# Odd and end stages of a two-layer streaming encoder: x in three loads, y in three parts, U turned from T, causal masks made later in place

## The chip, the cores and the metric

The program runs on one core of one Trainium2 chip. The metric is the device time of one execution in microseconds (us); lower is better. All arrays are float32. TensorE multiplies float32 operands as they are (a product of two float32 tiles is recorded as two matmuls), and operands that were rounded to the `fp32r` form as one.

## The reference

One inference step of a two-layer encoder on 320 tokens: 256 of a prompt and 64 of a sample, in chunks of 64. The width is 1024.

```python
def _swiglu(h, wg, wu, wd):
    return (jax.nn.silu(h @ wg) * (h @ wu)) @ wd        # 1024 -> 2816 -> 1024
# layer 0: x += 0.5 * swiglu(rmsnorm(x)); x += mix_even(rmsnorm(x)); x += 0.5 * swiglu(rmsnorm(x))
# layer 1: x += 0.5 * swiglu(rmsnorm(x)); x += mix_odd(rmsnorm(x));  x += 0.5 * swiglu(rmsnorm(x))
```

`mix_even` is a sparse softmax attention beside a gated linear attention; the change doesn't touch it. `mix_odd` is a gated delta rule with 8 heads of 128. In it, for each chunk of 64 tokens and each head:

```python
decay = jnp.exp(jnp.where(incl, gcum[..., :, None] - gcum[..., None, :], -jnp.inf))
lower = jnp.where(strict, jnp.einsum('bhtd,bhsd->bhts', kb, kc) * decay, 0.0)
sol = lax.linalg.triangular_solve(eye + lower, rhs, left_side=True, lower=True, unit_diagonal=True)
attn = jnp.where(incl, jnp.einsum('bhtd,bhsd->bhts', qc, kc) * decay, 0.0)
```

What follows is a recurrence over the chunks with the state of each head.

## The kernel before

x is held turned, as xT with the 1024 features in 8 tiles of 128 partitions and the 320 tokens along a row. Five engines run their own instruction streams, written out by hand and tied by semaphores: SyncE (SP) issues the loads of weights, ScalarE (ACT) rounds each weight tile to a high part, VectorE (DVE) or GpSimd (POOL) subtracts to get the low part, and TensorE (PE) does each product as three matmuls: high by high, high by low, low by high (L592 to L594 in the four FFNs, L677 to L679 in the odd layer's input projection).

**Start.** `prologue` on SP loads x of the prompt in one DMA (L521) and of the sample in another (L522), both counted by one semaphore, then gate and up weights of tile 0; the second pair waits until eleven small parameter rows have landed. PE waits for the whole of x, turns it with 24 transposes (L572), then turns the parameter rows (L576 to L578). ACT copies all six banks to xT, then the parameters, then rounds the gate weights, then makes h_hi (L1399). DVE makes h_lo (L1840) and the low weight parts (L1828). The first FFN's row norm needs the sum of squares over the features: ACT squares (L1405) and DVE sums the 8 tiles in one reduction (L1882) behind the low parts of weight tile 1. PE's `norm` (L587) stands between the products of weight tiles 0 and 1 and waits for that sum.

**Odd layer.** PE's loop over 32 weight tiles t is `project_odd(t)` and, behind it, pieces of the delta rule. T is the inverse of (1 + lower) and U is T turned; both are kept. Each of the five chunks starts from a first 2x2 level and is refined five times, which gives 25 steps m (chunk m % 5, level m // 5). A step is: Y = level mask of L times U (`inverse_y`, L1111, in bank 4), ACT copies Y (`y_out`), then T -= Y' T in bank 6 (L1126) and U -= T' Y in bank 7 (L1133), in `inverse_tu`; DVE subtracts both (`update`, L2315 and L2317). In the last level (m of 20 to 24) only U is refined. Steps stand one to a t at t = 14 to 23, two to a t at 24 to 28, and the rest at 29 to 31.

POOL makes for each t the low weight parts (`split_mix`, L2517) and masks (`masked`, L2586): the causal mask of the decays Dm into a tile At of its own at t = 11 to 15, the first level of T at t = 12 to 16 (`lev0`), and the level mask of step m = t - 12, which goes over Dm, so it waits for the causal mask. DVE's `lower` (L2285) reads Dm, `first_t` (L2291) waits for the first level, and `queries` (L2303) multiplies At at t = 19 to 23. PE's `key_products` (L1073, L1074) waits for `lower` of the chunk before, and `first_inverse` (L1097) turns T for the first U.

**End.** The last FFN's down product runs over 8 output tiles; DVE adds each to xT (L1868, L1872). Then `epilogue`: PE waits for the last tile and turns all of xT (24 transposes, L1253), ACT copies six banks to ytok (L1279), and POOL stores y of the prompt and of the sample in two DMAs (L2457) and waits for them.

## Time and profile before

| what | value |
|---|---|
| median of 3 timed runs | 1511.71 us (1511.51 to 1513.51) |
| profiled execution, device time | 1505.85 us |
| its span, first to last instruction | 1504.1 us |
| mean granted TensorE clock | 0.98 of full |
| PE busy | 1436.9 us (96% of the span) |
| DVE, ACT, POOL busy | 879.3, 603.3, 355.9 us |

Busy time is the time in which an engine has an instruction under way; a matmul's record begins before the one ahead ends, so the distance from start to start is what one costs in a row of them. Idle time in brackets stands before the instruction and names what ended it. The granted clock is 1.00 at 2.4 GHz and 0.50 at 1.2 GHz. The profiled execution is 5.86 us below the median of the timed runs.

### The profile page before, as it was taken

The numbers are of one execution on the slowest core, as the hardware profiler recorded it, in microseconds if no ns is written. First come the engines' busy times: TensorE is split into PE (matmuls) and PEld (weight loads), VectorE is DVE, ScalarE is ACT, GpSimd is POOL, SyncE is SP. The second block draws the span as 40 slices with busy tenths as digits, with TensorE's granted clock in tenths as the row PEclk, the third lists the DMA queues.
The fourth block names the chain that finished last, engine by engine and source line by source line (L and its number), as shares of the span: only waits on it lengthen the run. The fifth ranks groups of instructions, "written<-read, shape, count | busy, mean of one in ns | idle before, by whom it ended". The sixth has DMA issues, their size and how long they took to land.

```text
span 1504.1 us, 25482 instructions
## 1 busy us (share of the span) xinstructions
PE 1436.9 (96%) x9830; PEld 1400.1 (93%) x9830; DVE 879.3 (58%) x1388; ACT 603.3 (40%) x990; POOL 355.9 (24%) x341
## 2 busy tenths in 40 slices
PE   6999998999879999999999999999999889999997
PEld 5999998899868999999999999988999779999997
DVE  4666653477755666655666655667564456666641
ACT  5333323546533533332533332557432544333321
POOL 3000023656205200003100002549465242000000
PEclk8999999999979999999999999989999999999999
DMA  7655951344402455774455674212221222555751
GB/s 182 167 140 149 279 145 31 112 121 126 134 1 76 126 160 142 201 186 106 114 162 143 172 215 115 81 59 85 79 63 57 87 85 82 160 150 140 182 154 35
DMA packets 323307, 188.21 MB, mean 125 GB/s; under 512 B 10874, under 2 KB 320632, under 8 KB 323244
## 3 DMA queue, kind: packets, MB, share of 16 engines
q1 hardware_dynamic: 321088, 181.95, 43.9%
q0 software_dynamic: 1568, 5.29, 1.2%
q8 instruction: 42, 0.69, 0.2%
q10 hardware_dynamic: 588, 0.12, 0.0%
q14 instruction: 21, 0.17, 0.0%
HBM read 183.22 MB, written 4.11 MB: 125 GB/s over the span
## 4 chain that ended last, share of the span: by engine, by line
PE 87%; DVE 6%; ACT 4%; issue 2%; POOL 1%; DMA 0%; ACTq 0%; SPq 0%
PE PS L592 21%; PE PS L593 20%; PE PS L594 20%; PE PS L677 2%; PE PS L679 2%; PE PS L678 2%; PE PS L1133 1%; PE PS L1111 1%; PE PS L696 1%; PE PS L650 1%; PE PS L697 1%; PE PS L698 1%; PE PS L651 1%; PE PS L652 1%; PE PS L1126 1%
## 5 line engine op out<-in xcount | busy, mean ns | idle before, releaser
L592 PE MATMUL PS<-h_hi,w_parts 128*128 128x320 f32 x1408 | 438.8, 312 | 7.8 <-DVE h_lo L1840 7.8
L594 PE MATMUL PS<-h_hi,w_parts 128*128 128x320 f32 x1408 | 436.5, 310 | 0.0
L593 PE MATMUL PS<-h_lo,w_parts 128*128 128x320 f32 x1408 | 436.5, 310 | 0.0
L592 PEld LDWEIGHTS PS<-h_hi,w_parts 128*128 128x128 f32 x1408 | 265.9, 189 | 9.6 <-issue 7.9
L593 PEld LDWEIGHTS PS<-h_lo,w_parts 128*128 128x128 f32 x1408 | 265.9, 189 | 0.4 <-issue 0.2
L594 PEld LDWEIGHTS PS<-h_hi,w_parts 128*128 128x128 f32 x1408 | 265.6, 189 | 0.0
L1279 ACT ACTIVATE w_parts<-gu 128x1024 fp32r<-128x1024 f32 x176 | 176.7, 1051 | 160.2 <-PE PS L594 159.0
L1828 DVE TENSOR_TENSOR w_parts<-gu,w_parts 128x1024 fp32r<-128x1024 f32 x176 | 209.0, 1228 | 16.4 <-ACT w_parts L1279 16.2
L592 PE MATMUL PS<-act_hi,w_parts 128*128 128x320 f32 x704 | 217.5, 309 | 0.0
L593 PE MATMUL PS<-act_lo,w_parts 128*128 128x320 f32 x704 | 217.5, 309 | 0.0
L594 PE MATMUL PS<-act_hi,w_parts 128*128 128x320 f32 x704 | 217.5, 309 | 0.0
L2517 POOL TENSOR_TENSOR w_mix<-gu,w_mix 128x512 fp32r<-128x512 f32 x116 | 154.5, 1343 | 124.0 <-ACT w_mix L1279 123.8
L1279 ACT ACTIVATE w_parts<-dn 128x1408 fp32r<-128x1408 f32 x64 | 84.8, 1373 | 183.6 <-PE PS L594 183.6
L592 PEld LDWEIGHTS PS<-act_hi,w_parts 128*128 128x128 f32 x704 | 132.2, 188 | 0.0
L593 PEld LDWEIGHTS PS<-act_lo,w_parts 128*128 128x128 f32 x704 | 132.2, 188 | 0.0
L594 PEld LDWEIGHTS PS<-act_hi,w_parts 128*128 128x128 f32 x704 | 132.2, 188 | 0.0
L1392 ACT ACTIVATE rs<-rs 128x320 f32<-128x320 f32 x88 | 41.5, 472 | 203.0 <-DVE rs L1853 203.0
L1828 DVE TENSOR_TENSOR w_parts<-dn,w_parts 128x1408 fp32r<-128x1408 f32 x64 | 118.3, 1888 | 7.3 <-ACT w_parts L1279 7.1
L2505 POOL TENSOR_TENSOR RB<-xT 128x320 f32<-128x320 f32 x5 | 3.6, 721 | 495.2 <-DVE xT L1872 482.2
L1279 ACT ACTIVATE w_mix<-gu 128x512 fp32r<-128x512 f32 x116 | 72.0, 630 | 121.1 <-PE PS L679 68.2
L1859 DVE TENSOR_TENSOR rs<-rs,PS 128x320 f32<-128x320 f32 x88 | 42.9, 487 | 130.5 <-PE PS L594 130.1
L1868 DVE TENSOR_TENSOR rs<-PS,RB 128x320 f32<-128x320 f32 x32 | 15.7, 491 | 144.5 <-PE PS L594 144.5
(378 smaller groups left out, 2383.7 us busy)
## 6 DMA issues: line engine op xcount, KB each, us to landing
gu<-in_ffn_w_gate SPq DMA_DIRECT2D x88, 512.0 KB, 4.0
gu<-in_ffn_w_up SPq DMA_DIRECT2D x88, 512.0 KB, 5.2
dn<-in_ffn_w_down SPq DMA_DIRECT2D x32, 1408.0 KB, 7.1
gu<-in_od_w_in SPq DMA_DIRECT2D x32, 512.0 KB, 5.1
gu<-in_ev_w_in SPq DMA_DIRECT2D x26, 512.0 KB, 4.8
dn<-in_ev_w_out SPq DMA_DIRECT2D x4, 1024.0 KB, 5.3
dn<-in_od_w_out SPq DMA_DIRECT2D x4, 1024.0 KB, 5.0
RB<-bias_rows POOLq DMA_DIRECT2D x2, 576.0 KB, 7.7
```

What stands on the lines that cost most here:

```text
L592: mm(out, w_hi, hi, start=first, stop=False)
L593: mm(out, w_hi, lo, start=False, stop=False)
L594: return mm(out, w_lo, hi, start=False, stop=last)
L677: mm(out, w_hi, h_hi[:, k, :], start=(k == 0), stop=False)
L678: mm(out, w_hi, h_lo[:, k, :], start=False, stop=False)
L679: ins = mm(out, w_lo, h_hi[:, k, :], start=False, stop=(k == KT - 1))
L1279: return act_(out, in_, ACT.Copy, scale=scale)
L1392: act_(tanh_g[:, slot, :], gated[:, slot, :], ACT.Tanh, scale=0.5).then_inc(tanh_done, 1)
L1828: tt(w_parts[:, slot, 1, w], raw[:, slot, w], w_parts[:, slot, 0, w].bitcast(F32), ALU.subtract)\
L1859: tt(gated[:, slot, :], gated[:, slot, :], bank(2 * slot + 1, T), ALU.mult).then_inc(act_done, 1)
L1868: tt(tanh_g[:, slot, :], bank(4 + slot, T), rstd, ALU.mult).then_inc(act_mid, 1)
L2517: po.tensor_tensor(mix_parts(n, t)[:, 1, w].rearrange("p (k c) -> p k c", k=4), raw[:, 4 * half:4 * half + 4, :], mix_parts(n, t)[:, 0, w] ...
```

## The change

x comes in three loads with a semaphore each, and PE turns each part as it lands. The six banks are copied by ACT (lower halves) and DVE (upper halves). The 32 FFN gains get a semaphore, a transpose and a bank of their own, and the other parameters are copied later. ACT rounds the first gate weights behind two tiles of h_hi; DVE sums the squares with three adds, ahead of weight tile 1, and `norm` adds the last two tiles on PE. In the odd layer `inverse_tu` becomes `inverse_t`, which keeps one product a step, and `inverse_turn`, two steps later, which turns T into U for m below 20; DVE copies U from bank 7. The level masks get a tile of their own (where Dm was), Dm moves to where At was, and the causal mask is made in place at t = 17 to 21. At the end xT is turned in three parts: tiles 0 to 3 ahead of the last down product, 4 to 6 in its middle, 7 behind it; SP stores the three parts of the prompt and two of the sample, and ACT the last of the sample.

```diff
-            sp.dma_start(xnat[:, 0:2, :], I["x_prompt"][0].rearrange("(i p) d -> p i d", p=P)).then_inc(x_in, 16)
-            sp.dma_start(xnat[0:TS, 2, :], I["x_sample"][0]).then_inc(x_in, 16)
+            for i in range(2):
+                sp.dma_start(xnat[:, i, :], I["x_prompt"][0, i * P:(i + 1) * P, :]).then_inc(x_in[i], 16)
+            sp.dma_start(xnat[0:TS, 2, :], I["x_sample"][0]).then_inc(x_in[2], 16)
             load_gu(0)
-            sp.wait_ge(params_in, 16 * 11)
+            sp.wait_ge(params_in, 16 * 10)
...
+            for evacs, c0, c1 in ((11, 0, 512), (14, 512, 896)):
+                sp.wait_ge(pro_evac, evacs)
+                store(y_rows[:, :, c0:c1], ytok[:, :, c0:c1])
+                store(O["y_sample"][0][:, c0:c1], ysample[0:TS, c0:c1])
+            sp.wait_ge(pro_evac, 16)
+            store(y_rows[:, :, 896:D], ytok[:, :, 896:D])
...
             def prologue():
                 pe.wait_ge(consts, 1)
-                pe.wait_ge(x_in, 32)
                 for i in range(3):
+                    pe.wait_ge(x_in[i], 16)
...
-                pe.wait_ge(params_in, 16 * 11)
+                pe.wait_ge(gains_in, 16)
+                tr(bank(7)[:, 0:32], rs[0:32, 0:P], ident[0:32, 0:32]).then_inc(pro_pe, 1)
+                pe.wait_ge(params_in, 16 * 10)
...
                     pe.wait_ge(first_total, 1)
-                else:
-                    pe.wait_ge(total_ready, r)
+                    mm(bank(6, T), ones[:, :], squares[:, 0, :], start=True, stop=False)
+                    mm(bank(6, T), ones[:, :], squares[:, 1, :], start=False, stop=True).then_inc(norm_sum, 1)
+                    return
...
+                        if m == KT - 1 and k == FT // 2:
+                            turn_out(1)
...
+                if f == 3:
+                    down(0, KT - 2, 0)
+                    turn_out(0)
+                    down(1, KT - 1, 0)
+                    turn_out(2)
...
+            def turn_out(part):
+                tiles = (range(0, 4), range(4, 7), range(7, 8))[part]
+                pe.wait_ge(x_upd, X_FFN[3] + 3 + tiles[-1])
+                if part == 2:
+                    pe.wait_ge(pro_evac, 11)
+                for i in range(3):
+                    rows = P if i < 2 else TS
+                    for k in tiles:
+                        ins = tr(bank(y_bank(part, i))[0:rows, (k - tiles[0]) * P:(k - tiles[0] + 1) * P],
+                                 xT[:, k, i * P:i * P + rows], ident[:, :])
+                    ins.then_inc(pro_pe, 1)
...
-                        inverse_tu(t - 14)
+                        inverse_t(t - 14)
+                    if 16 <= t < N_CONV:
+                        inverse_turn(t - 16)
...
                             if m < 25:
-                                inverse_tu(m)
+                                inverse_t(m)
+                            if m - 2 < 4 * NCH:
+                                inverse_turn(m - 2)
...
+            def inverse_t(m):
                 c = m % NCH
                 pe.wait_ge(o["y_evac"], m + 1)
                 if m >= NCH:
                     pe.wait_ge(o["t_upd"], m - NCH + 1)
+                if m:
+                    pe.wait_ge(o["t_upd"], m)
+                else:
+                    pe.wait_ge(o["kt_evac"], NCH)
+                for p in range(C_PAIRS):
+                    left, right = yT[:, m % 2, p, :], tT[:, c, p, :]
+                    if m >= 4 * NCH:
+                        left, right = right, left
+                    ins = mm(bank(6)[:, p * P:(p + 1) * P], left, right, start=True, stop=True)
+                ins.then_inc(o["t_pe"], 1)
+            def inverse_turn(m):
+                pe.wait_ge(o["t_upd"], m + 1)
                 if m:
                     pe.wait_ge(o["u_upd"], m)
                 else:
                     pe.wait_ge(o["u1_evac"], 2)
                 for p in range(C_PAIRS):
-                    ins = mm(bank(7)[:, p * P:(p + 1) * P], tT[:, c, p, :], yT[:, m % 2, p, :], start=True, stop=True)
+                    ins = tr(bank(7)[:, p * P:(p + 1) * P], tT[:, m % NCH, p, :], ident[:, :])
                 ins.then_inc(o["u_pe"], 1)
...
# ACT
+                    sc.wait_ge(pro_pe, 2 * i + 1)
+                    copy(xT[:, 0:4, i * P:i * P + n_], bank(2 * i).rearrange("p (k c) -> p k c", k=4)[:, :, 0:n_])\
+                        .then_inc(pro_evac, 1)
...
+                        if f == 0 and k == 1:
+                            split_gate_up(0, 0, 0, 0, (0,))
...
                 if f == 0:
                     split_gate_up(0, 0, 0, 0, (1,))
+                    other_params()
...
                 def y_out(m):
                     sc.wait_ge(o["y_pe"], m + 1)
                     if m >= 2:
-                        sc.wait_ge(o["u_pe"], m - 1)
+                        sc.wait_ge(o["t_pe"], m - 1)
...
# DVE
+                if f == 0:
+                    low_parts(0, gain, range(2))
+                    split_half(0, gu, 0, 0, 0, 0)
+                    low_parts(0, gain, range(2, KT))
+                    split_half(0, gu, 0, 0, 0, 1)
+                    for j in range(1, 4):
+                        ve.wait_ge(sq_done, j + 1)
+                        ins = tt(squares[:, 0:2, :], squares[:, 0:2, :], squares[:, 2 * j:2 * j + 2, :], ALU.add)
+                        if j < 3:
+                            link(ins)
+                    ins.then_inc(first_total, 1)
...
+                def inverse_update(m):
                     c = m % NCH
+                    matrix = (tT if m < 4 * NCH else uT)[:, c, :, :]
+                    ve.wait_ge(o["t_pe"], m + 1)
+                    tt(matrix, matrix, bank(6).rearrange("p (a c) -> p a c", a=4), ALU.subtract).then_inc(o["t_upd"], 1)
+                def u_turned(m):
                     ve.wait_ge(o["u_pe"], m + 1)
+                    cp(uT[:, m % NCH, :, :], bank(7).rearrange("p (a c) -> p a c", a=4)).then_inc(o["u_upd"], 1)
...
# POOL
-                masked(Dm[:, c, :, :], Lm[:, c, :, :], lev[:, m // NCH + 1:m // NCH + 2, :], o["bm"])
+                masked(level[:, c, :, :], Lm[:, c, :, :], lev[:, m // NCH + 1:m // NCH + 2, :], o["bm"])
...
-                if 11 <= t < 16:
-                    c = t - 11
-                    po.wait_ge(o["dexp"], c + 2)
-                    masked(At[:, c, :, :], Dm[:, c, :, :], maskI.unsqueeze(1), o["am"])
...
                 if 12 <= t < N_CONV:
-                    if t < 17:
-                        po.wait_ge(o["am"], t - 11)
                     level_mask(t - 12)
+                if 17 <= t < 22:
+                    masked(At[:, t - 17, :, :], Dm[:, t - 17, :, :], maskI.unsqueeze(1), o["am"])
...
```

## Rows read from the trace of the kernel before

**Rows 1.** The page: share of the chain that ended last, by engine.

```profile
PE 87%; DVE 6%; ACT 4%; issue 2%; POOL 1%; DMA 0%; ACTq 0%; SPq 0%
```

**Rows 2.** Timeline of the start: start us, length us, engine, line, idle before.

```profile
7.75 4.31 PE L572 MATMUL PS<-ident,RA 128*128 128x128 f32 x24 [7.75 <-DMA RA<-in_x_sample]
13.91 1.25 DVE L1828 TENSOR_TENSOR w_parts<-gu,w_parts 128x1024 fp32r<-128x1024 f32 x1 [13.91 <-ACT w_parts L1279]
15.77 0.61 PE L592 MATMUL PS<-h_hi,w_parts 128*128 128x320 f32 x1 [3.37 <-DVE h_lo L1840]
21.24 0.47 PE L594 MATMUL PS<-h_hi,w_parts 128*128 128x320 f32 x1
21.51 0.38 PE L592 MATMUL PS<-h_hi,w_parts 128*128 128x320 f32 x1
...
24.18 4.53 DVE L1882 TENSOR_REDUCE RB<-RA 128x320 f32<-128x2560 f32 x1
25.24 0.31 PE L593 MATMUL PS<-h_lo,w_parts 128*128 128x320 f32 x1
25.39 0.31 PE L594 MATMUL PS<-h_hi,w_parts 128*128 128x320 f32 x1
28.85 1.41 PE L587 MATMUL PS<-RB,ones 128*128 128x320 f32 x2 [3.15 <-DVE RB L1882]
29.59 0.94 PE L592 MATMUL PS<-h_hi,w_parts 128*128 128x320 f32 x1
```

**Rows 3.** DMA issues: operation, engine, count, size, us from issue to landing.

```profile
gu<-in_ffn_w_up SPq DMA_DIRECT2D x1, 512.0 KB, 8.7
out_p_gla<-RB POOLq DMA_DIRECT2D x1, 128.0 KB, 2.2
out_y_sample<-RA POOLq DMA_DIRECT2D x1, 256.0 KB, 4.9
```

**Rows 4.** Odd layer, chain of waits in order of time: start, length, engine, line.

```profile
1122.33 0.89 PE PS L1111 x8
1123.27 1.13 PE PS L1126 x8
...
1165.67 0.87 PE PS L1145 x8
```

**Rows 5.** Stretches: length, busy us of PE, PEld, DVE, ACT, POOL, granted clock, DMA, GB/s.

```profile
29.00:34.00 5.00, 5.00 (x24) 4.61 (x25) 0.82 (x2) 3.11 (x5) 0.00 (x0) 0.71 1.06 235
1050.00:1080.00 30.00, 30.00 (x241) 29.99 (x240) 18.56 (x38) 13.00 (x31) 17.53 (x14) 1.00 0.24 71
1079.00:1084.00 5.00, 5.00 (x25) 5.00 (x25) 0.17 (x1) 0.96 (x2) 1.28 (x1) 0.66 0.00 0
```

**Rows 6.** DVE groups of 1008 to 1187 us: busy, mean ns, idle before.

```profile
L2315 DVE TENSOR_TENSOR RA<-RA,PS 128x512 f32<-128x512 f32 x20 | 13.7, 683 | 12.4 <-PE PS L1133 12.3
```

**Rows 7.** Timeline of POOL, DVE and PE in the odd layer.

```profile
1022.55 1.32 POOL L2586 TENSOR_TENSOR RB<-RB 128x512 f32<-128x512 f32 x1
...
1030.97 0.49 PE L1073 MATMUL PS<-RB 128*128 128x128 f32 x2 [0.77 <-DVE RB L2285]
1038.11 0.49 PE L1073 MATMUL PS<-RB 128*128 128x128 f32 x2 [1.59 <-DVE RB L2285]
1038.58 1.75 DVE L2291 TENSOR_TENSOR RA<-ident,RA 128x512 f32<-128x512 f32 x1 [0.52 <-POOL RA L2586]
1045.73 0.63 PE L1097 MATMUL PS<-ident,RA 128*128 128x128 f32 x4 [1.17 <-DVE RB L2285]
...
1169.41 1.13 PE L1111 MATMUL PS<-RB 128*128 128x128 f32 x8 [1.08 <-issue]
```

**Rows 8.** Timeline of the end.

```profile
1491.60 0.49 DVE L1868 TENSOR_TENSOR rs<-PS,RB 128x320 f32<-128x320 f32 x1 [8.66 <-PE PS L594]
1496.66 0.74 POOL L2457 DMA_DIRECT2D out_y_prompt<-RA  x1 [238.33 <-ACT RA L1279]
1497.40 0.55 POOL L2457 DMA_DIRECT2D out_y_sample<-RA  x1
```

More of the change, by code:

```diff
@@ L324, in mix_parts, with y_bank @@
             return w_mix[:, t % 2, :, :]
+        def y_bank(part, i):
+            return ((0, 1, 2), (3, 6, 7), (0, 1, 2))[part][i]
         def odd_bank(t):
@@ L1245, in recurrence @@
                 turn(NCH - 1, 1)
-            def epilogue():
-                pe.wait_ge(x_upd, X_FFN[3] + 2 + KT)
-                for i in range(3):
-                    rows = P if i < 2 else TS
-                    for half in range(2):
-                        for k in range(4):
-                            ins = tr(bank(2 * i + half)[0:rows, k * P:(k + 1) * P],
-                                     xT[:, 4 * half + k, i * P:i * P + rows], ident[:, :])
-                        ins.then_inc(pro_pe, 1)
             prologue()
@@ L1263, in _ @@
             ffn(3)
-            epilogue()
         @block.scalar
@@ L1299, in prologue, with other_params @@
                     n_ = P if i < 2 else TS
-                    for half in range(2):
-                        sc.wait_ge(pro_pe, 2 * i + half + 1)
-                        copy(xT[:, 4 * half:4 * half + 4, i * P:i * P + n_],
-                             bank(2 * i + half).rearrange("p (k c) -> p k c", k=4)[:, :, 0:n_]).then_inc(pro_evac, 1)
+                    sc.wait_ge(pro_pe, 2 * i + 1)
+                    copy(xT[:, 0:4, i * P:i * P + n_], bank(2 * i).rearrange("p (k c) -> p k c", k=4)[:, :, 0:n_])\
+                        .then_inc(pro_evac, 1)
                 sc.wait_ge(pro_pe, 7)
-                copy(cols[:, 0:C_QN], bank(6, 222)[:, 0:C_QN])
+                copy(cols[:, 0:32], bank(7, 32)).then_inc(pro_evac, 1)
+            def other_params():
+                sc.wait_ge(pro_pe, 8)
+                copy(cols[:, 32:C_QN], bank(6, 222)[:, 32:C_QN])
                 copy(cols[:, C_QN:C_QN + 1], bank(6, 222)[:, C_QN:C_QN + 1], A_D ** -0.5)
@@ L1770, in epilogue @@
             def epilogue():
-                for i in range(3):
-                    n_ = P if i < 2 else TS
-                    for half in range(2):
-                        sc.wait_ge(pro_pe, 7 + 2 * i + half + 1)
-                        copy(ytok[0:n_, i, half * 512:(half + 1) * 512], bank(2 * i + half)[0:n_, :])\
+                for part, c0, c1 in ((0, 0, 512), (1, 512, 896)):
+                    for i in range(3):
+                        sc.wait_ge(pro_pe, 8 + 3 * part + i + 1)
+                        n_ = P if i < 2 else TS
+                        copy((ytok[:, i, c0:c1] if i < 2 else ysample[0:TS, c0:c1]), bank(y_bank(part, i))[0:n_, 0:c1 - c0])\
                             .then_inc(pro_evac, 1)
+                sc.wait_ge(pro_pe, 16)
+                copy(ytok[:, :, 896:D], banks(0, 2, P)).then_inc(pro_evac, 1)
+                sc.wait_ge(pro_evac, 16)
+                sc.dma_start(O["y_sample"][0][:, 896:D], ysample[0:TS, 896:D]).then_inc(y_out, 16)
             prologue()
-            split_gate_up(0, 0, 0, 0, (0,))
             ffn(0, C_FFN, 0)
@@ L2345, in odd @@
                     if 14 <= t < N_CONV:
-                        update(t - 14)
+                        inverse_update(t - 14)
+                    if 16 <= t < N_CONV:
+                        u_turned(t - 16)
                     if t in (17, 18):
@@ L2355, in odd @@
                             if m < 25:
-                                update(m)
+                                inverse_update(m)
+                            if m - 2 < 4 * NCH:
+                                u_turned(m - 2)
                 gate_silu(31)
@@ L2436, in _ @@
             ve.sem_inc(act_split, 2)
-            split_half(0, gu, 0, 0, 0, 0)
+            for i in range(3):
+                n_ = P if i < 2 else TS
+                ve.wait_ge(pro_pe, 2 * i + 2)
+                cp(xT[:, 4:8, i * P:i * P + n_], bank(2 * i + 1).rearrange("p (k c) -> p k c", k=4)[:, :, 0:n_])\
+                    .then_inc(pro_evac, 1)
             ffn(0, C_FFN)
```

62 lines of the change are left out of this document (24 added, 38 removed).

## The prediction

> **What bounds the kernel now.** The chain of waits gives PE 87% of the span and every other engine together 11% [rows 1], so time is to be had in two ways: work taken off PE where it runs without a gap, and gaps of PE closed. I read the timeline of the first 40 us and of the last 15, then busy time by stretches of the odd layer, then the timeline of each engine where PE has gaps there. The reader is to see three places.
>
> At the start PE waits until 7.75 for the whole of x, again 3.37 us until 15.77, and 3.15 us at 28.85 for the sum of squares [rows 2]. From 15.77 matmuls stand 0.27 apart (21.24 to 21.51) and later 0.15 (25.24 to 25.39) [rows 2]; the first is the clock at 1.2 GHz. After the wait at 28.85 it is low again: the mean grant of 29 to 34 is 0.71, which is 2.9 of 5 us at half [rows 5].
>
> In the odd layer PE is busy all of 1050 to 1080 us, DVE 18.56 of 30 and POOL 17.53 [rows 5]: what leaves PE there leaves the span. Only before 1046 has it gaps, 0.77, 1.59 and 1.17 us, each behind DVE's `lower` [rows 7]; DVE in turn sits in `first_t` until POOL's mask (1038.58, idle 0.52 [rows 7]), and POOL has three masks of about 1.3 us and two weight parts for each t.
>
> At the end nothing overlaps: the last product ends at 1491.55, DVE starts at 1491.60, POOL issues y at 1496.66 and 1497.40 [rows 8], the last lands 4.9 later [rows 3], at 1502.3, and the span closes 1.8 after that.
>
> **The change, part by part.** Minus is faster.
>
> *x in three loads, copies on two engines.* What ended the second wait was not x but the order on ACT: six copies, parameters, gate rounding, then h_hi. With x0 landing first (1 MB lands 5.5 after issue, so half of it near 5) PE turns it before x1 is there, at the same 4.31 us for 24 [rows 2] spread over the landings, ends near 9.2, and ACT, with three copies instead of six, has two tiles of h_hi by about 10.7. Next it wants the weights, and waits for both halves of them: up was issued at 2.56 and lands 8.7 later, 11.3 [rows 3]. SP now has one more x DMA of about 0.5 us ahead, but the DMA engines are full until 10.6, so I put landing at 11.4 (bounds 11.3 and 11.8). Then rounding 1.1, DVE's low part 1.25 [rows 2] and two semaphore steps: PE starts at 13.95 instead of 15.77, **−1.8** (bounds −1.4 and −2.1). The low tiles 2 to 7 of h come 0.45 apart where PE takes 0.8 a tile, so they are not late. SP's second weight pair waits for ten parameter rows and not eleven, the last of them the same one as before: nothing.
>
> *Sum of squares.* The reduction of 4.53 stood behind two low parts of 1.2 [rows 2]. Now three adds of 640 elements, about 0.9 each by the 128x320 operations of 0.49 [rows 8], follow the squares as they come and end near 20.6. PE ends weight tile 0 at 13.95 + 9.8 = 23.7, so the wait is gone: 25.54 to 28.85, **−3.3**. `norm` is two float32 products instead of one: the one cost 28.85 to 29.59, 0.74 at the low clock [rows 2], so two at the high clock cost 0.74: nothing. Without the gap the clock should not fall; PE was slow for 2.1 us of the products behind 29.59, **−1.0** (bounds 0 and −1.4). What is late next: rstd, at 24.4 + 2.3 = 26.8, the activation of tile 0 by 29.5 and the low half of tile 2 by 31.1, against PE's need of it at 31.5. That is 0.4 to spare; if it is missed, some tenths. Start in all: **−6.1** (−3.5 to −7).
>
> *U turned from T.* A product of a step is 0.89 [rows 4]; four transposes are half of the eight in 0.87, 0.44 [rows 4]. Products go from 45 (20 of T, 25 of U) to 25, transposes of T come in for 20 of the steps: 20 x 0.89 = 17.8 off, 20 x 0.44 = 8.7 on, of which one 0.44 falls in the gap of 1.08 at t = 29 [rows 7]. **−9.5**. At 24 to 28, where two steps share a t, the second T product came 0.05 late and took 1.13 for 0.89 [rows 4], since DVE's update of T waited for U's product as well. Now DVE starts a semaphore (0.2 to 0.3) after T's product, takes 0.68 [rows 6], and PE has a turn and a Y, 1.33, in between: five times 0.27, **−1.3**. DVE trades a subtraction of 0.68 for a copy of about 0.69 of the same shape: nothing. The new wait, `inverse_turn` for T's update, stands two steps behind it; behind it in PE's queue are the next projection and the next Y, and Y wants the U of five steps ago, copied in the t before, 3.5 us of projection earlier. The price of these waits lies between 0 and, if each t lost the 1.33 between DVE and PE, +20; I take 0, since each is released a t earlier.
>
> *Causal masks later.* POOL loses one mask of 1.32 [rows 7] at each of t = 11 to 15, where it was late, and gets it at 17 to 21, where its load by t becomes 4 x 1.28 = 5.1 against PE's 6.65. DVE's `first_t` comes up to 1.4 earlier, but ACT's two table loads at t = 12 and its own order let only 0.46 through to `lower(2)` and 0.93 to `lower(4)`. Of the gaps 0.77 shrinks to 0.31 and 1.17 to 0.70; the 1.59 stays: **−0.9** (bounds 0 and −3.5, all three gaps). Odd layer in all: 9.5 + 1.3 + 0.9 = **−11.7** (−6 to −14).
>
> *y in three parts.* 21 of 24 transposes move ahead of the last product's end: 21 x 0.109 [rows 4] = +2.3, a move only. From that end: DVE 1.1, three transposes 0.5, a copy 0.5, a semaphore, issue at +2.3; the last store is 128 KB, which took 2.2 elsewhere [rows 3], ACT's small one a little more: +4.7, against 10.75 before (1491.55 to 1502.3). 4.7 − 10.75 + 2.3 = **−3.8** (−2.5 with a landing of 3.5; −4.5 at the best). The first two parts are copied and stored under the last product, 9.7 us long.
>
> *A rule against it.* The 0.109 apart of L1145 is the rate of a full clock, and PE came to those transposes from products [rows 4]; the trace has no stretch made mostly of them. The Trainium skill (TensorE: Matmul & The Clock Gate, Part 4: PE-mode transpose) says that a transpose doesn't count as activity of PE for the clock gate. By that rule the added ones invite falls of the clock; by the rows they don't, and the sum stays. I keep the rule's case as a rival.
>
> **The sum.** −6.1 − 11.7 − 3.8 = −21.6 on 1505.85, the profiled execution, which gives 1484.3. The median of the runs lies 5.86 higher; no part of the change should alter what lies between, so I predict 1511.7 − 21.6 = **1490 us**, 1.4% less.
>
> **Rivals.**
> 1. *PE isn't the bound in the odd layer once its load is less.* Then the shorter steps turn into waits for DVE, whose own work by t is about 5.5 us, or for ACT's copies of Y. For: PE did wait for DVE before 1046 [rows 7]. Against: 18.56 of 30 busy [rows 5]. Half of −9.5 lost and −0.9 too: 1490 + 5.7, about 1496.
> 2. *The start gives only its first part.* The clock stays low longer after an earlier, cold start, or rstd is late for tile 2: of −6.1 some −2.5 is left, and y's landing is 1 us longer: about 1494.5.
> 3. *The clock falls oftener.* After the 20 one-column sums before 1079 the mean grant of 1079 to 1084 was 0.66 [rows 5], which costs 5 x 0.34 = 1.7. If the turns bring a fall at each t of 16 to 31, 16 x 1.7 = 27 more: 1490 + 27 = 1517, slower. It decides from 13 falls on. For: the clock did fall in a busy stretch. Against: products stay most of each t. One or two falls more or less, at either sign, are likely: ±3.4.
> 4. *The change doesn't do what it says*, some moved wait ends where the old one did in all three places: no change, 1511.
>
> **How the numbers follow.** Forecast 0.68 (its own range 1486 to 1495), rival 1 0.13, rival 2 0.13, rival 3 0.03, rival 4 0.03. Less than 0.2%, 3 us, can't be told from no change here. Faster 0.94, same 0.03, slower 0.03. The range for 8 in 10 goes from the best bounds with a fall of the clock less, 1484, to rival 1 with a fall more, 1499.
>
> **What would show it.** The first product near 14, `norm` with no wait and the next product near 24.4; L1133 gone, t = 24 to 28 about 8.0 apart instead of 9.2, and 14 to 23 0.45 to 0.9 shorter; PE's three gaps before 1046 down by about 0.9 together; stores issued 2.3 after the last product and a span that ends 6.5 after it instead of 12.6. Waits of PE for DVE or ACT in the odd layer at t of 16 on, or low clock there in new places, would make it wrong.

## The result, and the profile after

The changed kernel takes 1484.24 us (median of 4 runs, 1483.85 to 1486.27) against 1511.76 for the kernel before, a ratio of 0.9829 [0.981, 0.9849]. The profiled execution took 1483.85 us, 22.0 less than the profiled one of before (1505.85): the sum of the prediction was 21.6. The medians differ by 27.5. The 5.5 between the two figures are not shown to be the change's work, and they have experiments of their own below.

The page of the changed kernel, its span, the share of PE, and the chain by engine: PE's share of the chain goes from 87% [rows 1] to 89%, and PE is busy for 96% of the span.

```profile
span 1482.1 us, 25338 instructions
PE 1427.7 (96%) x9753; PEld 1391.3 (94%) x9753; DVE 877.1 (59%) x1394; ACT 602.1 (41%) x989; POOL 356.7 (24%) x339
PE 89%; DVE 5%; ACT 4%; issue 2%; DMA 0%; ACTq 0%
```

**The start** (timeline of the changed kernel: start, length, engine, line, idle before). It answers to [rows 2].

```profile
4.70 4.14 PE L590 MATMUL PS<-ident,RA 128*128 128x128 f32 x24 [4.70 <-DMA RA<-in_x_prompt]
11.50 1.06 ACT L1320 ACTIVATE w_parts<-gu 128x1024 fp32r<-128x1024 f32 x1 [1.15 <-DMA gu<-in_ffn_w_up]
12.59 1.23 DVE L1878 TENSOR_TENSOR w_parts<-gu,w_parts 128x1024 fp32r<-128x1024 f32 x1 [1.64 <-ACT w_parts L1320]
13.91 0.60 PE L614 MATMUL PS<-h_hi,w_parts 128*128 128x320 f32 x1 [2.84 <-issue]
17.82 2.54 DVE L1932 TENSOR_TENSOR RA<-RA 128x640 f32<-128x640 f32 x3
22.94 0.70 PE L605 MATMUL PS<-RA,ones 128*128 128x320 f32 x2
23.78 0.55 PE L614 MATMUL PS<-h_hi,w_parts 128*128 128x320 f32 x1
```

PE turns the first part of x at 4.70 where it stood until 7.75; the first product is at 13.91 for 15.77. The three adds end at 20.4, before PE asks at 22.94, so `norm` waits for nothing, and the next product stands at 23.78 for 29.59. A mark below is the start of the same group of PE's instructions in two traces. Every later mark up to the odd layer is 6.8 to 6.9 earlier than before (the even layer's first turn 257.4 to 250.6, first odd projection 961.6 to 954.7). Some tenths of that belong to the execution: a second profiled execution of the changed kernel (experiment 8) has its first turn of the even layer at 251.3, one of the kernel before (experiment 1) at 258.1.

**The odd layer** (timeline of PE in the changed kernel at one t of the second half: Y, T, turn, Y, T, turn; then two of DVE's groups of 990 to 1171 us, with busy time, mean ns, idle before). Before, a step had a T and a U product, each of the size of the Y product of 0.89 [rows 4].

```profile
1129.09 1.05 PE L1157 MATMUL PS<-RB 128*128 128x128 f32 x8
1129.98 1.06 PE L1174 MATMUL PS<-RA,dn 128*128 128x128 f32 x8
1130.87 0.60 PE L1185 MATMUL PS<-ident,RA 128*128 128x128 f32 x4
1131.31 1.06 PE L1157 MATMUL PS<-RB 128*128 128x128 f32 x8
1132.42 1.13 PE L1174 MATMUL PS<-RA,dn 128*128 128x128 f32 x8
1133.38 0.60 PE L1185 MATMUL PS<-ident,RA 128*128 128x128 f32 x4
```

```profile
L2373 DVE COPY RB<-PS 128x512 f32<-128x512 f32 x20 | 13.6, 682 | 0.0
L2369 DVE TENSOR_TENSOR RA<-RA,PS 128x512 f32<-128x512 f32 x20 | 13.6, 679 | 4.7 <-PE PS L1174 4.7
```

The turn takes 0.44 (1130.87 to 1131.31), as its price said, and no wait stands ahead of it. DVE's copy of U costs 0.682 where a subtraction of that shape cost 0.683 [rows 6]. But the second T product of this t still starts late: Y ends at 1131.31 + 0.89 = 1132.20, T starts at 1132.42. It waits for DVE's update of T, and that one stood behind DVE's product of the output gate (timeline of DVE at this place):

```profile
1130.37 1.30 DVE L2281 SCALAR_TENSOR_TENSOR RB<-RA,RB 128x320 f32<-128x320 f32 x1 [0.59 <-ACT RA L1706]
1131.60 0.67 DVE L2369 TENSOR_TENSOR RA<-RA,PS 128x512 f32<-128x512 f32 x1
```

The T product ahead had ended at 1130.87. The same holds at two more of the five t; at one where DVE is free in time (update at 1106.60) the second T product starts without a wait. The t of 24 to 28 stand 8.0 to 8.3 apart, for 9.15 before. Before, PE had three gaps ahead of 1046, of 0.77, 1.59 and 1.17 us [rows 7]; now it has one:

```profile
1029.96 0.49 PE L1119 MATMUL PS<-RB 128*128 128x128 f32 x2 [1.37 <-DVE RB L2341]
```

From the first odd projection to the first new values the odd layer takes 212.1 us instead of 224.7, −12.6. The lead of the changed kernel is 6.89 at the first key product (1015.40 to 1008.51), 9.45 at the second Y (1046.19 to 1036.74), ahead of which no product of U stands, and 19.48 at the first new values: 2.6 are the masks' part and 10.0 that of U. Behind it a little is given back. Two stretches of the recurrence in the changed kernel (length, busy us of PE, PEld, DVE, ACT, POOL, granted clock, DMA, GB/s), and the only one of the kernel before, at 1226:

```profile
1168.00:1172.00 4.00, 3.98 (x26) 3.21 (x28) 1.02 (x3) 1.67 (x6) 0.00 (x0) 0.57 0.67 227
1206.00:1214.00 8.00, 6.55 (x28) 6.55 (x29) 1.56 (x4) 0.50 (x2) 0.46 (x1) 0.57 0.46 133
```

```profile
1226.00:1230.00 4.00, 4.00 (x17) 4.00 (x18) 0.00 (x0) 0.00 (x0) 0.00 (x0) 0.57 0.55 160
```

The lead is 19.5 at the first new values (1186.3 to 1166.9), 18.5 at the recurrence's last turn and 17.6 at the last FFN's products (1413.5 to 1395.9): 1.9 lost, across the two stretches at 1.2 GHz.

**The end** (timeline of the changed kernel, then its last DMA issues with size and us to landing). It answers to [rows 8].

```profile
1476.31 0.49 DVE L1918 TENSOR_TENSOR rs<-PS,RB 128x320 f32<-128x320 f32 x1 [10.96 <-PE PS L616]
1477.38 0.55 PE L673 MATMUL PS<-ident,xT 128*128 128x128 f32 x3 [1.11 <-DVE xT L1922]
1477.86 0.38 ACT L1320 ACTIVATE RB<-PS 128x256 f32<-128x256 f32 x1 [5.81 <-PE PS L673]
1478.28 0.38 SPq L568 DMA_DIRECT2D out_y_prompt<-RB  x1
1478.29 0.54 ACTq L1827 DMA_DIRECT2D out_y_sample<-hT  x1
```

```profile
out_y_prompt<-RB SPq DMA_DIRECT2D x1, 128.0 KB, 1.9
out_y_sample<-hT ACTq DMA_DIRECT2D x1, 32.0 KB, 2.1
```

From the last product (1476.27) the stores are issued after 2.0, land after 2.1 more, and the span ends at 5.9, where it was 12.6. Less the 2.3 of turns moved ahead of the product, that is −4.4.

By stages the 22.0 are: start −6.9, odd layer −12.6, given back +1.9, end −4.4.

### The profile page after: what moved, and what is told of

Same layout as the page of the kernel before. It is cut to its first block, busy times and chain, and to the rows that moved or that the text cites. A ratio compares the mean times of both kernels' runs of the same rounds, so it can differ in the third digit from the quotient of the medians.

```text
span 1482.1 us, 25338 instructions
## 1 busy us (share of the span) xinstructions
PE 1427.7 (96%) x9753; PEld 1391.3 (94%) x9753; DVE 877.1 (59%) x1394; ACT 602.1 (41%) x989; POOL 356.7 (24%) x339
## 4 chain that ended last, share of the span: by engine, by line
PE 89%; DVE 5%; ACT 4%; issue 2%; DMA 0%; ACTq 0%
PE PS L614 21%; PE PS L616 21%; PE PS L615 21%; PE PS L719 2%; PE PS L721 2%; PE PS L720 2%; PE PS L1174 2%; PE PS L1157 2%; PE PS L738 1%; PE PS L692 1%; PE PS L739 1%; PE PS L740 1%; PE PS L693 1%; PE PS L694 1%; DVE RA L2061 1%
## 5 line engine op out<-in xcount | busy, mean ns | idle before, releaser
L614 PE MATMUL PS<-h_hi,w_parts 128*128 128x320 f32 x1408 | 437.8, 311 | 7.2 <-DVE h_lo L1890 4.4
```

What stands on the lines that cost most here:

```text
L614: mm(out, w_hi, hi, start=first, stop=False)
```

## The experiments

Times are medians; "low" is the lowest of a kernel's runs. The kernel before ran 65 times over all comparisons: 19 executions took 1505.4 to 1507.5 us and 46 took 1510.5 to 1515, none between. The changed kernel ran 9 times: 1483.8 to 1488.1. The experiments ran on three chips (1 to 4 and 12 on one, 5 to 8 on a second, 9 to 11 on a third); each comparison had the kernel before on its own chip, with executions of both groups every time. Differences below are to the changed kernel's median of 1484.24, so where the two ran on different chips they carry that too. "Loss" is the time that PE had less of full clock: a fall of 3.4 us at 1.2 GHz is a loss of 1.7. The "even tail" of the expectations is the end of the even layer, about 375 to 484 us.

**1. The kernel before, unaltered.**

> The kernel before, unchanged, once more. The timed runs of before lie 5.9 us above its profiled execution (1511.71 against 1505.85), those of the changed kernel only 0.4 (1484.24 against 1483.85), so of the 27.5 us between the medians the two traces explain 22.0. Theory 1: the 5.9 us are inside the span, in executions in which something of the kernel before runs slower (the clock, a stage); then the spans of the timed runs are near 1510 and differ from 1504, and the profile taken here may show where. Theory 2: they lie outside the span (between launch and first instruction); then spans are near 1504 in all runs and only the device time differs, by 5 to 6 us more than the usual 1.7.

Measured 1511.42 (1506.43 to 1514.75, 12 runs), ratio 1.0003 [0.9987, 1.0018]; profiled execution 1511.56, with a span of 1509.8. The time outside the span is 1.7, as in the shorter ones (1505.85 with 1504.1), so the 5.7 lie inside. The marks agree within 0.9 up to the first turned values of the even tail (393.11 and 393.94), and differ by 5.8 from 425 on. Stretch 396 to 408 of the shorter execution, then of this one (granted clock behind POOL's column):

```profile
396.00:408.00 12.00, 11.13 (x94) 10.66 (x95) 11.20 (x28) 6.18 (x15) 2.73 (x4) 1.00 0.23 75
```

```profile
396.00:408.00 12.00, 10.99 (x58) 10.83 (x58) 7.80 (x18) 5.21 (x13) 1.27 (x2) 0.57 0.28 94
```

PE is as busy and does 58 instructions for 94, at 0.57: one fall of the clock more (396 to 406, 5.1 of loss), in the even layer, far from the change; the fall behind it is longer by 1.7. The prediction's 5.86 was a second group of executions, not a fixed part.

**2. U by a product again.** In `inverse_turn`'s place a product, at once and not two steps later, and DVE subtracts as before:

```diff
-                            if m - 2 < 4 * NCH:
-                                inverse_turn(m - 2)
+                            if m < 4 * NCH:
+                                inverse_turn(m)
...
-                pe.wait_ge(o["t_upd"], m + 1)
...
-                    ins = tr(bank(7)[:, p * P:(p + 1) * P], tT[:, m % NCH, p, :], ident[:, :])
+                    ins = mm(bank(7)[:, p * P:(p + 1) * P], tT[:, m % NCH, p, :], yT[:, m % 2, p, :], start=True, stop=True)
```

> The changed kernel with U refined by a product again (20 products of 0.89 in place of 20 turns of 0.44, DVE subtracts and waits for both products). By the sum of the prediction +9.5 and +1.3, so 10.8 slower than the changed kernel, near 1495. By rival 1 (PE is not the bound once its load is less) only about 5 slower, near 1489.

Measured 1496.05 (1495.74 to 1497.76, 6 runs), ratio 0.9907 [0.9888, 0.9926]: +11.8 on the changed kernel; between the profiled executions +12.3, of which the odd layer has +11.4. Of these, 1.5 came ahead of the first step, with a fall at 996 us that the changed kernel has not; 9.9 are left for U. PE of this kernel, at the same place as the T and turn above:

```profile
1131.79 1.06 PE L1173 MATMUL PS<-RA,dn 128*128 128x128 f32 x8
1132.68 1.06 PE L1183 MATMUL PS<-dn,RA 128*128 128x128 f32 x8
```

The turning of U is the largest term and PE is the bound there: what left PE left the span (20 times 0.89 less 0.44 is 9.0). Rival 1, which had half of it lost, falls.

**3. The causal masks early again.**

```diff
                     po.wait_ge(o["kk_used"], c + 1)
+                    masked(At[:, c, :, :], Dm[:, c, :, :], maskI.unsqueeze(1), o["am"])
                     masked(tT[:, c, :, :], Lm[:, c, :, :], lev[:, 0:1, :], o["lev0"])
...
-                if 17 <= t < 22:
-                    masked(At[:, t - 17, :, :], Dm[:, t - 17, :, :], maskI.unsqueeze(1), o["am"])
```

> The changed kernel with the causal masks made at t = 12 to 16 again, in place, ahead of T's first level, so that POOL has three masks a t there. By the prediction +0.9 (1485.1) out of PE's gaps before the first products; by the rival that POOL held all three gaps up, up to +3.5 (1487.7); no change if DVE and ACT alone set those gaps.

Measured 1487.15 (1486.75 to 1491.16, 5 runs), ratio 0.9852 [0.9829, 0.9875]: +2.9. PE's gaps in this kernel:

```profile
1023.78 0.49 PE L1119 MATMUL PS<-RB 128*128 128x128 f32 x2 [0.76 <-DVE RB L2341]
1030.93 0.49 PE L1119 MATMUL PS<-RB 128*128 128x128 f32 x2 [1.60 <-DVE RB L2341]
1038.50 0.63 PE L1143 MATMUL PS<-ident,RA 128*128 128x128 f32 x4 [1.12 <-DVE RB L2341]
1047.26 1.13 PE L1174 MATMUL PS<-RA,dn 128*128 128x128 f32 x8 [1.50 <-DVE RA L2369]
```

The three gaps of [rows 7] are back within 0.05 (0.76, 1.60, 1.12 for 0.77, 1.59, 1.17), with a fourth behind them that the kernel before did not have: 4.98 of waiting where the changed kernel has 1.37. The odd layer is 4.1 longer here; its falls are elsewhere (one of 3.4 us at 1073 more, the one at 984 shorter by as much), and the rest of the time moves with the clock's falls too. Masks that are early cost this kernel about 3 us. What the change itself gained by moving them is less, since the fourth gap is not in the kernel before: 2.2 of waits (3.53 to 1.37), 2.6 by the marks, not 0.9.

**4. The end as before**: all turns behind the last product, two stores by POOL.

```diff
-                        if m == KT - 1 and k == FT // 2:
-                            turn_out(1)
...
-                    down(0, KT - 2, 0)
-                    turn_out(0)
-                    down(1, KT - 1, 0)
-                    turn_out(2)
...
```

> The changed kernel with the end as before: all of xT turned behind the last product, six copies by ACT, two stores by POOL. By the prediction +3.8; by the difference of the two traces from the last FFN on, +4.4, so about 1488.5. If the two stores' landing hides behind something the change would be under 2.

Measured 1493.94, ratio 0.9884 [0.9863, 0.9906]; one run of 1488.62 and five of 1493.0 to 1494.7. Against the changed kernel's 1484.2 that is +4.4 or +8.8 to 10.4. The profiled one is of the longer kind (1494.67): it has a fall at 389 to 399 us, and stands 5.8 behind the changed kernel at the output projection (457.7 for 451.9), where nothing that this kernel alters has run yet; 1.1 of it was there at the even layer's first turn. Its end alone:

```profile
1480.41 0.49 DVE L1890 TENSOR_TENSOR rs<-PS,RB 128x320 f32<-128x320 f32 x1 [8.67 <-PE PS L604]
1485.48 0.74 POOL L2492 DMA_DIRECT2D out_y_prompt<-RA  x1 [239.34 <-ACT RA L1296]
```

From DVE's start to the span's end (1493.0) are 12.6, in the changed kernel 5.8. Less the 2.3 of turns that now stand inside it, the end is worth 4.5. In the profiled execution the rest is the clock's; that the other longer runs have the same fall is not shown.

**5. The sum of squares late again**: DVE's one reduction behind weight tile 1, one `norm` product.

```diff
-                    for j in range(1, 4):
-                        ve.wait_ge(sq_done, j + 1)
-                        ins = tt(squares[:, 0:2, :], squares[:, 0:2, :], squares[:, 2 * j:2 * j + 2, :], ALU.add)
...
+                if f == 0:
+                    ve.wait_ge(sq_done, 4)
+                    ve.tensor_reduce(total, squares.rearrange("p k t -> p t k"), AX, ALU.add).then_inc(first_total, 1)
```

> The changed kernel with the sum of squares as before: DVE's one reduction behind weight tile 1, and `norm` one product. Theory: PE reaches `norm` at 22.9 us and DVE's low parts of tile 1 end near 22.4, so the reduction of 4.53 ends near 27.0: PE waits 4.0, and behind the wait the clock is low again, 1.0 more; together +4 to +5 on the changed kernel's 1484.2, about 1488.7, and every later mark of PE that much later. Rival, the wait at 28.85 was hidden or is paid back later: 1484 to 1485.5. Second rival: the shift moves the falls of the clock in the even layer, and the time is 5 to 6 us more on top of the theory (1494), with the marks equal to the theory's up to the place of the added fall.

Measured 1493.54 (1489.04 to 1495.88, 6 runs), ratio 0.9885 [0.9864, 0.9906]. PE in this kernel:

```profile
27.13 1.41 PE L607 MATMUL PS<-RB,ones 128*128 128x320 f32 x2 [3.30 <-DVE RB L1933]
28.60 0.47 PE L613 MATMUL PS<-h_lo,w_parts 128*128 128x320 f32 x1
28.87 0.47 PE L614 MATMUL PS<-h_hi,w_parts 128*128 128x320 f32 x1
```

The wait is there, and behind it products stand 0.27 apart, the pace of 1.2 GHz, until 33. The even layer starts at 257.0 for 250.6: +6.4, of which 0.3 was there at the first product (14.18), 3.3 is the wait and the rest, about 3, the low clock. The lowest run is 5.3 above the changed kernel's lowest. Theory right in kind, small in size: the low clock cost more than the 1.0 it was given. The median carries the second rival as well: the profiled execution has the fall at 395 to 405.

**6. x whole**: one more loop of waits ahead of the first transpose.

```diff
+                for i in range(3):
                     pe.wait_ge(x_in[i], 16)
+                for i in range(3):
```

> The changed kernel with one edit: PE waits for all three parts of x before it turns the first. Theory, that the early turning of the first part is what brought the first product from 15.77 to 13.91: PE turns from about 7.8 (the last part's landing) to 12.0, ACT has two tiles of h_hi near 13.0, its gate rounding and DVE's low part follow, and the first product is at about 15.4: +1.5, 1485.7. Rival, that ACT's and DVE's shared copies did it and the landing of up (11.5) ends the wait anyway: the first product stays below 14.3 and the time within 0.4 of 1484.2.

Measured 1486.67 (1486.11 to 1488.78, 5 runs), ratio 0.9849 [0.9828, 0.987]: +2.4.

```profile
7.78 4.69 PE L591 MATMUL PS<-ident,RA 128*128 128x128 f32 x24 [7.78 <-DMA RA<-in_x_sample]
16.30 0.61 PE L615 MATMUL PS<-h_hi,w_parts 128*128 128x320 f32 x1 [2.83 <-DVE w_parts L1879]
```

The first product moves from 13.91 to 16.30. The even layer's first turn is 2.3 later too. The early turning gives all of the first term and more; with x whole, the other edits of the start together bring the first product no earlier than before (16.30 for 15.77).

**7. The first gate weights on a semaphore of their own**, an attempt at a better kernel.

```diff
-            load_gu(0)
+            for (dst, src), landed in zip(gu_source(0), (y_out, gu_loaded[0])):
+                sp.dma_start(dst, src).then_inc(landed, 16)
...
-                            split_gate_up(0, 0, 0, 0, (0,))
+                            sc.wait_ge(y_out, 16)
+                            copy(w_parts[:, 0, 0, 0:1024], gu[:, 0, 0:1024]).then_inc(hi_done, 1)
```

> The changed kernel, and one thing more: the first gate weights have a semaphore of their own, so that ACT rounds them when they have landed, without waiting 1.15 us for up's. Theory, that this wait is the last one before the first product: ACT's rounding starts near 10.4 instead of 11.50, the first product near 12.8 instead of 13.91: -1.1 us, 1483.1. Rival, that gate and up land together (both share the DMA engines with x): 0. Second rival: PE starts earlier and stays at the low clock up to the same moment, so that half of it is lost: -0.5.

Measured 1483.84 (1483.25 to 1489.27, 5 runs), ratio 0.9827 [0.9806, 0.9848]. ACT's rounding starts at 10.76 for 11.50 and the first product stands at 13.16 for 13.91, but the low run is only 0.5 under the changed kernel's, and the intervals can't tell the two apart. PE's own marks say why: the clock's first lasting rise comes at 18.1 us in the changed kernel's profile, at 19.6 in its second one (experiment 8) and at 19.4 here, and PE reaches `norm` at 22.94, 23.69 and 23.07. The lead of 0.75 at the first product is gone there, and two executions of one kernel differ by as much. Inconclusive; if there is a gain it is half a microsecond.

**8. The changed kernel, unaltered.**

> The changed kernel, nothing altered, to see how its own times spread. The kernel before has executions of 1506 to 1507.5 (5 of 29) and of 1510 to 1515, and the profiled ones of either kind differ by one more fall of TensorE's clock in the even layer, 396 to 407 us. Theory, that each program has its own place in that pattern, set by when PE's gaps fall: most executions of the changed kernel within 1483.8 to 1486.3, none or few at 1489 to 1490. Rival, that the split is a matter of the chip or of the moment: one in three or more of them 5 to 6 us above the lowest.

Measured 1486.53 (1483.78 to 1488.11, 5 runs), ratio 0.9838 [0.9816, 0.9861]: two at 1484, one at 1486.5, two at 1488.1. The profiled one (1488.11) has a clock of 0.976 for 0.979; its falls at 412 and 453 are longer by 1.7 of loss each, others come at 487 and 1245, and one at 1211 is shorter by 1.7. It has no fall at 388 to 400: what makes this execution of the changed kernel longer is not the one fall of experiment 1. Neither expectation holds as it stood. (The kernel before had 7 of 29 executions below 1508 by then, not 5.) Kernels whose first 950 us are instruction for instruction those of the changed one (experiments 2, 3, 4 and 8, with the first four runs) had 0 of 6, 1 of 5, 5 of 6 and 2 of 9 executions 4 us or more above their lowest. It looks as if a kernel leans to one side, by something other than the code ahead of the place; so few runs of each don't show it.

**9 and 10. Two gaps of the even tail filled.** Two of PE's gaps stand just ahead of the place where the extra fall begins in experiments 4, 5 and 7 (388 to 395). Here PE does work there whose results are never read, by products and by transposes of the same time.

```diff
+                keep_busy(bank(3)[:, 0:P], 6)
                 token_rows("k", (3, 4, 5), T_K, s["ktr"])
                 value_turns()
+                pe.wait_ge(s["l_done"], 3)
+                keep_busy(bank(7)[:, 0:P], 7)
                 key_turns()
```

With transposes the two numbers are 12 and 14, and `keep_busy` transposes instead of multiplying.

> The changed kernel with PE kept busy in its two gaps of the even tail between 384.6 and 389.3 us (1.65 and 1.76 us, each behind a copy of ACT): 6 products of 128x128 (0.22 each) between the token rows of v and those of k, 7 between the turned values and the turned keys, their results never read. Theory, that the extra fall at 388 to 400 us, which makes some executions 4 to 6 us longer than others, is brought on by these gaps: no execution has it, all within 1483.5 to 1485.5, and PE's later marks stand where the shorter executions have them (gla scores 390.4). Rival, that the extra fall comes from something else of the moment: two of five or more still at 1487 to 1490. Second rival: the products run past the end of the gaps and cost up to 0.5.

> The same two gaps filled for the same time by transposes, 12 and 14 of 0.109. From 381.8 to 390.4 PE then does transposes without a pause, and nothing else. Theory, that a busy PE is what holds the clock, whatever the instruction: as with the products, no extra fall, 1483.5 to 1485.5. Rival, the rule of the Trainium skill (TensorE: Matmul & The Clock Gate, Part 4: PE-mode transpose), that a transpose doesn't count as activity for the clock gate: the extra fall comes as often as in the changed kernel or in every execution, two of five or more at 1487 to 1490.

Measured with products 1485.54 (1483.61 to 1489.24, 6 runs), ratio 0.9839 [0.9814, 0.9864], two of six at 1488 or more with a clock of 0.976; with transposes 1486.65 (1484.22 to 1486.97, 5 runs), ratio 0.9837 [0.9811, 0.9863], none above 1487. The gaps went from 1.65 and 1.76 us to 0.2 to 0.3 each, and the spread stayed: three of six and three of five executions lie above the 1485.5 of the theory. The theory that these two gaps make the longer executions falls. Whether they bring on the fall at 388 is not shown: neither profiled execution (1486.98 and 1486.86) has it, but neither has one of the two of the changed kernel; both have a longer fall at 413 and others at 488 and 1242 instead. The two kernels can't be told apart by so few runs. One thing the trace with transposes does show: from 382.9 to 391.5 PE does 70 transposes and nothing else, at a granted clock of 1.00, and the next fall comes at 412.8, as with products (413.0).

**11 and 12. Six gaps of the even tail filled** (five by the expectation's count). Also behind the column sums, ahead of and behind the first turn of the sample, and ahead of the output projection, where each profiled execution of the changed kernel has falls; again with products, then with transposes.

```diff
                 gla_sums()
+                keep_busy(bank(3)[:, 256:384], 12)
                 turn(3)
...
                 scores_sample()
+                pe.wait_ge(s["pt_evac"], 4)
+                keep_busy(bank(3)[:, 256:384], 17)
                 turn_sample(0)
+                keep_busy(bank(4)[:, 256:384], 6)
                 turn_sample(1)
...
                 values_sample(3)
+                keep_busy(bank(3)[:, 256:384], 7)
```

> As with the products in the two gaps, and also in the later gaps of the even tail where every execution has a fall of the clock: 12 products behind the column sums (gap of 3.21 to 416.55), 17 ahead of the first turn of the sample (4.22 to 436.56), 6 behind it, 7 ahead of the output projection. Theory, that these falls (414 to 422, 434 to 446, 450 to 456 us) come from the gaps and cost what PE does at half clock inside the chain: 2.6 + about 3 + 1.5, so 1484.2 - 7 = about 1477, with a granted clock of 1.00 from 384 to 484. Rival, that DVE's and ACT's work sets that stretch and the clock only fills it: -2, 1482. Second rival: a fall comes later instead, in the projection or the FFN, where PE is the bound, and takes the gain back: 1484 or more.

> All five gaps of the even tail filled as in the version with products (1481.2), but by transposes of the same total time (12, 14, 24, 34, 12 and 14 of 0.109 us). Every execution of the changed kernel falls to half clock behind three of these gaps, and the products took those falls away (412 to 484 us: one of 1.7 us of loss left of 10.2). Theory, that a busy PE holds the clock whatever the instruction: the same, 1481 within 1. Rival, the Trainium skill's rule (TensorE: Matmul & The Clock Gate, Part 4: PE-mode transpose), that transposes don't count as activity for the clock gate: the falls at 414 to 422, 434 to 446 and 450 to 456 come back, and the time is the changed kernel's, 1484 to 1486.

Measured with products 1481.19 (1479.41 to 1485.22, 6 runs), ratio 0.981 [0.9786, 0.9835]; with transposes 1480.47 (1479.16 to 1482.42, 5 runs), ratio 0.9808 [0.9787, 0.9828]. Ten of these eleven executions are below the lowest of the changed kernel's nine (1483.78): these versions beat the changed kernel, by 3 to 5 us. The kernel before had its usual times beside them (medians 1511.5 and 1511.1). Three stretches of the changed kernel, then of the one with products, then with transposes (PE busy, ..., granted clock):

```profile
434.00:440.00 6.00, 2.43 (x10) 1.95 (x11) 5.74 (x16) 3.24 (x8) 0.00 (x0) 0.55 0.00 0
440.00:446.00 6.00, 6.00 (x30) 5.27 (x29) 1.78 (x6) 3.56 (x8) 0.27 (x1) 0.60 0.02 4
452.00:458.00 6.00, 6.00 (x32) 6.00 (x33) 3.91 (x5) 1.26 (x2) 0.34 (x1) 0.75 0.78 240
```

```profile
434.00:440.00 6.00, 5.41 (x46) 4.97 (x45) 5.72 (x16) 3.87 (x10) 0.00 (x0) 1.00 0.00 0
440.00:446.00 6.00, 4.63 (x34) 3.83 (x32) 1.95 (x6) 5.29 (x11) 2.60 (x2) 1.00 0.01 4
452.00:458.00 6.00, 6.00 (x43) 6.00 (x42) 2.11 (x3) 1.10 (x2) 1.24 (x2) 1.00 0.85 283
```

```profile
412.00:418.00 6.00, 6.00 (x42) 6.00 (x41) 3.04 (x5) 1.70 (x4) 0.00 (x0) 0.72 0.00 0
434.00:440.00 6.00, 4.98 (x40) 4.20 (x39) 5.39 (x17) 4.11 (x10) 0.00 (x0) 1.00 0.00 0
440.00:446.00 6.00, 4.78 (x37) 4.11 (x35) 2.17 (x2) 5.39 (x8) 3.85 (x2) 1.00 0.02 4
452.00:458.00 6.00, 6.00 (x43) 6.00 (x42) 2.17 (x3) 2.01 (x2) 2.42 (x3) 1.00 0.65 206
```

Where PE was kept busy the clock stayed at 2.4 GHz, with transposes as with products. From 430.5 to 437.8 the version with transposes has PE do 56 transposes and nothing else; it has no fall from 416.5 to 979.8. Only the fall that begins at 413 (415 with products), right behind the 20 one-column sums, is left, shortened from 6.8 to 3.4 us. At the output projection the lead is 3.6 us with transposes (451.9 to 448.3; 0.5 of it from the start) and 2.3 with products, which had started 0.7 late: 3.1 and 3.0 gained, where 7 was expected. At full clock PE waits for DVE's softmax and ACT's copies (4.63 and 4.78 busy of 6 at 440), as the first rival said, and a fall comes back in the odd layer (5.1 us of loss at 978 to 994, for 3.4 in the changed kernel).

## Why the prediction came out

The mechanism was right in all three places. The sum on the profiled execution came within half a microsecond (−21.6 for −22.0), and that is partly luck: the three places gave 23.9, 2.3 more than predicted, and 1.9 of it was lost again behind the odd layer. The time, 1490, was 5.8 too high for one reason that is no term of the sum. At 1484.24 the result lies just inside the range of 8 in 10 (1484 to 1499) and below the forecast's own (1486 to 1495); the changed kernel's lowest runs, 1483.78, lie below both.

- *The offset of 5.86, "no part of the change should alter what lies between".* This step failed. The 5.86 were the distance between two groups of executions of the kernel before, one more fall of the clock in the even tail (experiment 1); its median lay in the longer group. The changed kernel has no such group: its nine executions spread over 4.3 us, and the four of the comparison lay mostly at the low end. Low against low, 1505.44 and 1483.78, the change is −21.7.
- *x and copies, −1.8.* Right (13.91 for 13.95 predicted), and experiment 6 puts 2.4 on the early turning. ACT could start on the weights at 11.50, for the 11.4 of the prediction.
- *Sum of squares −3.3, clock −1.0.* The wait is gone. Taken out alone it is worth 5.3 in time, low against low, and 6.4 at the even layer's start. The term that was too small is the clock's, close to 3 in experiment 5. The start as a whole gave 6.9 for 6.1, of which up to 0.7 can be the execution's. rstd was not late (PE has no wait from 23 to 45 us), and rival 2 falls.
- *U turned, −9.5, with stalls −1.3.* Together 10.8 predicted, 10.0 by the marks of the change, 9.9 by experiment 2. The stalls were not the way described: DVE no longer waits for U's product, but three of the five second T products still start 0.22 behind Y and cost 0.3, as before, since DVE's update stands behind its gate product of 1.3. So of −1.3 about 0.5 came. The waits of `inverse_turn` cost nothing.
- *Masks, −0.9.* Mis-sized: PE's waits there went from 3.53 to 1.37, and the marks give 2.6. The gaps of 0.77 and 1.17 vanished where 0.31 and 0.70 were to be left, and the one that was to stay at 1.59 is 1.37; so more came through to `lower` than the 0.46 and 0.93 that the prediction put down to ACT. What holds the 1.37 was not taken apart. The bound of −3.5 held it.
- *The parts measured singly (11.4 and 4.1 in the odd layer) add to more than its 12.6*: 1.5 of the first is a fall ahead of the first step, and 1.7 of the second (by the marks) is the price of a fourth gap that the kernel before has not; less these the sum is 12.3.
- *Rival 3, falls.* Behind 1168 the changed kernel has 3.4 more of loss than the kernel before; the +1.9 in time are the "one or two falls" that rival 3 allowed. As a fall at each t it is refuted.
- *End, −3.8.* −4.4; the last small store landed in 2.1 and the tail behind the last product was 5.9 for 6.5.
- *The rule.* The prediction weighed the rows against a rule and kept the rows. The Trainium skill (TensorE: Matmul & The Clock Gate, Part 4: PE-mode transpose) says that the full clock doesn't engage in transpose mode, because a transpose doesn't count as a busy PE the same way. The runs here don't bear it out. Transposes held the clock: 56 of them and nothing else from 430.5 to 437.8 us, at 1.00 (experiment 12). They also raised it: at the start PE does nothing but transposes, and in the changed kernel the clock's record goes to 1.00 at 7.9 us in the midst of them. Both rows below begin with the sixteenth turn of x (timeline of PE, 8.15 to 8.8 us; the changed kernel, then experiment 2's, where the clock did not rise by then): nine turns in 0.92 us, seven in 1.25.

```profile
7.92 0.92 PE L590 MATMUL PS<-ident,RA 128*128 128x128 f32 x9
```

```profile
7.86 1.25 PE L590 MATMUL PS<-ident,RA 128*128 128x128 f32 x7
```

That rise does not come in every execution, and where it comes the clock falls again before the first product (11.3 us in the changed kernel), PE having been nearly idle since 8.9.

## What to carry to other kernels

Where PE is busy without a gap, count what leaves PE and believe the sum; a transpose in place of a second product is paid in full. Before a median is used as a base, look whether the executions fall into groups: here two groups of one kernel lie a quarter of the change apart, and one trace shows only one of them. A sum that comes out can hide terms that cancel: check it stage by stage. Gaps of PE in a latency-bound stretch cost twice, by themselves and by the clock behind them, and filling PE's idle time with unread work gave 3 to 5 us here.

## What the runs showed of the hardware

- The falls of the clock cost 1.7 us of full clock, or 3.4 or 5.1, in all these traces. From 40 us to the last product they are in total 22.2 in the shorter execution of the kernel before, 29.0 in the longer one, 25.6 in the changed kernel (1483.85), 18.8 with the six gaps filled by products, 17.1 by transposes. Whether a given one comes can differ between executions of one kernel (the fall at 396 in the kernel before). What decides it stays open.
- The column of the granted clock reads 1.00 wherever the trace has no record of the clock yet, whatever PE's pace. In experiment 6 the first record is a rise at 20.4 us; the stretch 18 to 20 reads 1.00, and its products stand 0.27 apart, as at 1.2 GHz: 9 in 2 us. The changed kernel's records begin at 7.9, and its stretch 14 to 18, with the same pace, reads 0.50. The totals above leave the start out for this reason.

```profile
18.00:20.00 2.00, 2.00 (x9) 2.00 (x9) 2.00 (x4) 2.00 (x6) 2.00 (x3) 1.00 0.00 0
```
